# Feed-forward gate and up projections by a seven-product form over quarters of the operands

## The reference, cut to what matters

```
xn2 = rms_norm(h, norm2_w)                       # (512, 1024)
h   = h + (silu(xn2 @ w_gate) * (xn2 @ w_up)) @ w_down   # w_gate, w_up: (1024, 2816)
out = rms_norm(h, final_norm_w)
```

## Time and profile before

| | |
|---|---|
| median of the runs | 874.74 us |
| span of the profiled execution | 873.0 us (its own time is not listed apart; the median less the span is 1.74 us) |
| TensorE busy | 859.7 us, 98% |
| VectorE (DVE), ScalarE (ACT), GpSimd (POOL) busy | 34%, 36%, 39% |
| mean granted TensorE clock | 0.998 |

### The profile page before, as it was taken

How to read it: one execution, slowest core, us unless ns; L and a number is a source line. 1 busy time by engine, 2 the same in 40 slices (tenths; PEclk the granted TensorE clock), 3 DMA queues, 4 the chain that set the end, 5 groups by cost and what they waited for, 6 DMA issues and landing times.

```text
span 873.0 us, 10397 instructions
## 1 busy us (share of the span) xinstructions
PE 859.7 (98%) x4078; PEld 715.1 (82%) x4078; DVE 297.8 (34%) x304; ACT 314.4 (36%) x313; POOL 337.9 (39%) x80
## 2 busy tenths in 40 slices
PE   8999999999999999999999999999999999999996
PEld 7888888788788888888888898888888888888885
DVE  6374428563473912121212333000000000444445
ACT  3532445654655623232322553222222222222233
POOL 4444443214224244444444525444444444444440
PEclk9999999999999999999999999999999999999999
DMA  8842212212112132222225212222222222222212
GB/s 322 270 174 96 98 49 97 72 72 96 38 58 96 47 98 96 96 96 96 96 96 217 96 50 97 96 96 96 96 96 96 96 96 96 97 96 96 96 48 97
DMA packets 14658, 89.82 MB, mean 103 GB/s; under 512 B 1712, under 2 KB 1968, under 8 KB 5296
## 3 DMA queue, kind: packets, MB, share of 16 engines
q1 hardware_dynamic: 12384, 82.32, 26.1%
q10 hardware_dynamic: 2256, 7.24, 2.4%
HBM read 87.46 MB, written 2.10 MB: 103 GB/s over the span
## 4 chain that ended last, share of the span: by engine, by line
PE 92%; DVE 3%; ACT 2%; issue 1%; DMA 1%; POOL 0%; DVEq 0%; ACTq 0%; POOLq 0%
PE bank L849 19%; PE bank L851 19%; PE bank L850 19%; PE bank L868 9%; PE bank L867 9%; PE bank L866 9%; PE bank L1009 1%; PE bank L995 1%; PE bank L1003 1%; PE bank L965 1%; DVE vgs L649 1%; DMA par<-cols 1%; PE bank L895 0%; ACT w_hi L306 0%; PE bank L896 0%
## 5 line engine op out<-in xcount | busy, mean ns | idle before, releaser
L259 POOL TENSOR_TENSOR w_lo<-raw,w_hi 128x2048 fp32r<-128x2048 f32 x71 | 327.1, 4607 | 484.9 <-ACT w_hi L306 484.9
L849 PE MATMUL bank<-xt_hi,w_hi 128*128 128x512 f32 (+1 forms) x704 | 269.6, 383 | 3.2 <-ACT yb L406 1.5
L851 PE MATMUL bank<-xt_hi,w_lo 128*128 128x512 f32 (+1 forms) x704 | 267.1, 379 | 0.0
L850 PE MATMUL bank<-xt_lo,w_hi 128*128 128x512 f32 (+1 forms) x704 | 267.1, 379 | 0.0
L306 ACT ACTIVATE w_hi<-raw 128x2048 fp32r<-128x2048 f32 x72 | 137.7, 1912 | 297.3 <-PE bank L851 157.1
L849 PEld LDWEIGHTS bank<-xt_hi,w_hi 128*128 128x128 f32 x704 | 132.4, 188 | 29.5 <-issue 3.2
L850 PEld LDWEIGHTS bank<-xt_lo,w_hi 128*128 128x128 f32 x704 | 132.4, 188 | 25.8 <-issue 1.0
L851 PEld LDWEIGHTS bank<-xt_hi,w_lo 128*128 128x128 f32 x704 | 132.4, 188 | 25.1
L790 DVE TENSOR_TENSOR act<-bank,sil 128x512 f32 (+1 forms) x22 | 15.2, 692 | 199.2 <-PE bank L851 199.2
L795 DVE TENSOR_TENSOR al<-act,ah 128x1024 fp32r<-128x1024 f32 x11 | 51.7, 4700 | 60.2 <-ACT ah L504 60.2
L866 PE MATMUL bank<-w_hi,ah 128*128 128x512 f32 x176 | 68.5, 389 | 0.0
(11 more groups left out here) (175 smaller groups left out, 950.6 us busy)
## 6 DMA issues: line engine op xcount, KB each, us to landing
raw<-wstream SPq DMA_DIRECT2D x72, 1024.0 KB, 4.8
xw<-x_t SPq DMA_DIRECT2D x4, 512.0 KB, 8.2
h<-x ACTq DMA_DIRECT2D x1, 2048.0 KB, 7.8
out<-h SPq DMA_DIRECT2D x3, 512.0 KB, 2.6
raw<-wstream SPq DMA_DIRECT2D x2, 512.0 KB, 5.8
xn_in<-x SPq DMA_DIRECT2D x2, 512.0 KB, 12.0
xn_in<-x ACTq DMA_DIRECT2D x2, 512.0 KB, 4.3
vbias_bc<-vbias ACTq DMA_DIRECT2D x1, 1024.0 KB, 7.8
```

What stands on the lines that cost most here:

```text
L259: pool.tensor_tensor(w_lo[s][:, :], raw[s][:, :], w_hi[s][:, :], ALU.subtract).then_inc(lo_ready, 1)
L849: pe.matmul(dst, wh[:, k, cs], rh[:, k, ts], start=(k == 0), stop=False)
L850: pe.matmul(dst, wh[:, k, cs], rl[:, k, ts], start=False, stop=False)
L851: last = pe.matmul(dst, wl[:, k, cs], rh[:, k, ts], start=False, stop=(k == KD - 1))
```

## The change

The first pair stays as it was. For each of the other ten, the product of the weight pair W (read as 2 x 2 quarters: contraction halves k 0-3 and k 4-7, by the tiles of each of the two column groups) with the activations X (2 x 2 quarters: contraction halves by halves of 256 tokens) is made by Strassen's form in the variant with seven products. The operands are A11, A12, A22 (quarters of W) and the sums S1 = A21 + A22, S2 = S1 - A11, S3 = A11 - A21, S4 = A12 - S2; on the side of X, T1 = B12 - B11, T2 = B22 - T1, T3 = B22 - B12, T4 = B21 - T2 are formed once. A product is two column groups by four contraction steps by three matmuls, 24 matmuls of 256 columns; a pair is 7 x 24 = 168 of them where it was 96 of 512 columns.

The weight pair is loaded raw by two DMAs of 1024 KB each (k 0-3 and k 4-7 of both blocks, `k1_landed`, `k2_landed`) into `wp`, which takes the place of `raw[0]` and `raw[1]`. The sums are formed in PSUM: ACT copies A21 into banks 6-7 (`diff`), DVE forms S1, S2, S4 in banks 4-5 (`chain`) and S3 in `diff`. ACT makes seven high parts a pair, DVE the four low parts of the sums, POOL the three of the plain quarters. Each of the seven operands has one buffer. The results are joined from banks 0 to 3 by DVE (five additions of 512 columns) and ACT (two copies) into `cq`, ACT takes `silu` of the gate half, and POOL multiplies (`gated_pair`). Preparation runs one pair ahead: while TensorE makes pair p, the other engines prepare pair p+1, except S4, whose parts are made at the start of its own pair.

```
 SP
+sp.wait_ge(hi_ready, B_DOWN); sp.wait_ge(lo_ready, B_DOWN)
+pair_half(.., 0, k1_landed); pair_half(.., 1, k2_landed)
+with sp.Fori(1, PAIRS) as i:
+    sp.wait_ge(op_high, i*7 + (1-7)); sp.wait_ge(plain_low, i*3 + (1-3)); sp.wait_ge(s_formed, i*4 + (3-4))
+    pair_half(wstream[pair i], 0, k1_landed)
+    sp.wait_ge(op_high, i*7 + (6-7)); sp.wait_ge(plain_low, i*3); sp.wait_ge(s_formed, i*4)
+    pair_half(wstream[pair i], 1, k2_landed)
 TensorE
+def pair(p, first=False):        # first: further waits on the T operands and on the banks
+    pe.wait_ge(op_high, p*7 + (1-7)); pe.wait_ge(plain_low, p*3 + (1-3)); pe.wait_ge(taken, p*2 - 2)
+    product("A11", x11, 0, True)
+    pe.wait_ge(s_low, p*4 + (1-4)); pe.wait_ge(joined, p*5 - 5)
+    product("S1", t1, 2, True)
+    pe.wait_ge(s_low, p*4 + (2-4)); product("S2", t2, 1, True)
+    pe.wait_ge(s_low, p*4 + (3-4)); product("S3", t3, 3, True)
+    pe.wait_ge(plain_low, p*3 - 1); pe.wait_ge(taken, p*2 - 1)
+    product("A12", x21, 0, False)
+    pe.wait_ge(plain_low, p*3); pe.wait_ge(joined, p*5 + (2-5))
+    product("A22", t4, 3, False)
+    pe.wait_ge(s_low, p*4); pe.wait_ge(joined, p*5 + (3-5))
+    product("S4", x22, 2, False)
 DVE, pair(p) in order
+    join_c12(p-1); s_low_of("S4", chain, p*7)
+    form_s1(p*16 + 16, p + 1)     # waits for a21_copied and k2_landed of pair p+1
+    s_low_of("S1", ..); form_s2(); form_s3()
+    join_u2(p); s_low_of("S2", ..); join_u3(p); join_c22(p)
+    s_low_of("S3", ..); form_s4(); join_c21(p)
 ACT, pair(p) in order
+    s_high("S4", ..) after product 7(p-1); a21_copy(p*16 + 16); pair_silu(p-1); take_p1(p)
+    plain_high("A11"); s_high("S1") after product S1; s_high("S2") after S2; s_high("S3") after S3
+    take_c11(p); plain_high("A12"); plain_high("A22") after product A22
 POOL
+a11_low(1); a12_a22_low(5, 6); a11_low(7 + 1); a12_a22_low(7 + 5, 7 + 6)
+with pool.Fori(2, PAIRS) as p:
+    gated_pair(p-1, p-1); a11_low(p*7 + 1); a12_a22_low(p*7 + 5, p*7 + 6)
```

More of the change, by code:

```diff
@@ L489, in _ @@
             normalise_h(3)
[L490 to L501, removed]
+            split_turned(2)
@@ new lines, in _, with pair_silu @@
+            t_split(1, tb_hi[1][:, :, :])
+            t_split(2, tb_hi[2][:, :, :])
+            gate(0)
+            gate(1)
+            s_high("S2", chain, 2)
+            a.wait_ge(up_done, 2)
+            s_high("S3", diff, 3)
+            plain_high("A12", slice(4, 8), slice(0, P), k2_landed, 16)
+            t_split(3, xt_hi[:, 0:4, HT:SEQ])
+            plain_high("A22", slice(4, 8), slice(P, 2 * P), k2_landed, 16)
+            s_high("S4", chain, 4)
+            def pair_silu(n):
+                a.wait_ge(joined, n * 5)
+                a.wait_ge(taken, n * 2)
+                a.activation(silp[:, :, :], cq[:, :, 0, :], ACT.Silu).then_inc(silp_ready, 1)
@@ L780, in _ @@
             rstd_h(3)
[L781 to L791, removed]
+            weigh_turned(2)
@@ new lines, in quarter, with join_c22, join_c21 @@
+            def quarter(n, b, u):
+                return v.tensor_tensor(cq[:, n, :, :], bank[b][:, :].rearrange("p (g t) -> p g t", g=2),
+                                       u[:, :].rearrange("p (g t) -> p g t", g=2), ALU.add)
+            def join_c22(p, first=False):
+                if not first:
+                    v.wait_ge(pair_ready, p - 1)
+                v.wait_ge(joined, p * 5 + (2 - 5))
+                quarter(3, 2, u3).then_inc(joined, 1)
+            def join_c21(p):
+                v.wait_ge(product_done, p * 7 + (6 - 7))
+                quarter(2, 3, u2).then_inc(joined, 1)
@@ new lines, in join_c12, with pair @@
+            def join_c12(p):
+                v.wait_ge(product_done, p * 7)
+                quarter(1, 2, u2).then_inc(joined, 1)
+            def pair(p, first=False):
+                if not first:
+                    join_c12(p - 1)
+                    s_low_of("S4", chain, p * 7)
+                v.wait_ge(s_low, p * 4)
+                form_s1(p * 16 + 16, p + 1)
+                s_low_of("S1", chain, p * 7 + 2)
+                v.wait_ge(s_low, p * 4 + 1)
+                form_s2()
+                form_s3()
+                join_u2(p)
+                s_low_of("S2", chain, p * 7 + 3)
+                join_u3(p)
+                join_c22(p, first)
+                s_low_of("S3", diff, p * 7 + 4)
+                v.wait_ge(s_low, p * 4 + 2)
+                form_s4()
+                join_c21(p)
@@ L1070, in _ @@
                 tile_T(bank[2 + t][:, s1], wk(w_hi, 1), wk(w_lo, 1), t, xt_hi, xt_lo, s1).then_inc(up_done, 1)
[L1071 to L1078, removed]
-                    tile_T(bank[2 + t][:, :], wk(w_hi, 1), wk(w_lo, 1), t, xt_hi, xt_lo).then_inc(up_done, 1)
+            x11 = (xt_hi[:, 0:4, 0:HT], xt_lo[:, 0:4, 0:HT])
@@ L1082, in down @@
+            pair(1, True)
+            with pe.Fori(2, PAIRS + 1) as p:
+                pair(p)
             def down(m, s, first=False, last=False):
```

332 lines of the change are left out of this document (278 added, 54 removed).

## The result

The changed kernel takes 875.9 us (median of 20 runs, 875.29 to 876.62); before stands at 874.74 (20 runs, 874.63 to 874.85) on the same chip. Ratio 1.0014, 95% interval [1.0008, 1.0021]: some 0.14% slower, within what I had called no change, and on the other side of the forecast of 874.3. The profiled execution took 875.68 us with a span of 873.6, where before the span is 873.0. So 0.6 us of the profiled execution's difference lies inside the span. The rest is outside it: time minus span is 2.05 to 2.15 us in all 20 runs, against 1.74 before; I don't know why.

The account below looks back on a forecast made before the run. TensorE, busy 98% of the span, was taken to bound the kernel. Products and initial wait -16.8, ring +4.2, first pair's wait +10.0, clock +2.2 sum to -0.4 us: 874.3 us, own range 871.5 to 877, overall 867.5 to 884.

Parts of the forecast that it names:

- The first of the ten: Wait ahead of A22 in the first Strassen pair, whose successor's second weight half is loaded late: +10.0 us, bounds 7 and 12.
- the 1.74 us between time and span: Difference between median and profiled span before, carried over unchanged: span 872.6 became median 874.3 us.
- Products: TensorE's ten pairs: 168 matmuls at 0.120 us instead of 96 at 0.227, -16.1 us, and 0.7 us less initial wait.
- Engine loads: No side engine overfull per pair of 20.16 us: DVE 13.2, ACT 10.6, POOL 9.6 us.
- The ring: Loop from product A22 through reloading the single second-half weight buffer to next A22: 20.7 against 20.16 us, eight times, +4.2 us.
- The interpolation between transfers of other sizes with the same rows: Second weight half's 1024 KB transfer with 4 KB rows: 5.0 us between 3.6 and 7.8; 4.9 taken, bounds 4.7 and 6.
- The rival: Ring longer: the second half lands in 6 us, +9.9, 884.2 us; decides against the change from 5.2 us on; chance 0.28.
- the lock: POOL and DVE collide where DVE has both inputs in SBUF, for a whole instruction; costs only in the preparation, not the loop.
- The tile copies of `act`, S2, S3 come in time: First pair: S2 and S3 (533.6, 534.8) ready for products at 533.7 and 536.6, so no wait there.
- one of the prediction's signs of being wrong: PE waiting elsewhere than ahead of A22 (ahead of S1 or S4), a DVE PSUM pass over 1.3 us, or pace not 0.120.
- The clock: After the first pair's 10 us wait TensorE's clock is down for some twenty matmuls: +2.2 us, bounds 0 and 3.9.
- The chances: Forecast 0.46, ring not binding 0.25, ring longer 0.28, weight loads 0.01; hence faster 0.33, slower 0.35, no change 0.32.

Follow-up runs that it names:

- halves_before: Kernel before, with each 512-column matmul of the ten pairs made as two of 256: 887.78 us, ratio 1.0150.
- act_order: three_lock, with ScalarE in the first pair taking C11 and making A12's and A22's high parts right behind S1's, ahead of S2's and S3's: 859.83 us, 0.9835.
- rows8k: Changed kernel, with each weight half laid out as one 8 KB row per partition instead of two of 4 KB: 870.86 us, 0.9953.
- rows_lock: rows8k, with DVE's preparation order changed to keep instructions on two SBUF inputs away from POOL's: 867.35 us, 0.9923.
- four_edits: rows8k plus u3 ahead of S2's low part, first pair's joins ahead of next S1, and early A12/A22 high parts in the preparation: 871.4 us, 0.9961.
- five_edits: four_edits, with POOL instead of DVE making the low parts of T2 and T3 in the preparation: 868.45 us, 0.9926.
- three_lock: three_edits plus the DVE preparation order of rows_lock: 865.61 us (4 runs), 0.9887.
- three_edits: rows8k plus u3 ahead of S2's low part and the first pair's joins ahead of the next S1: 865.61 us (4 runs), 0.9900.

## Why the prediction was off, step by step

The forecast was 874.3 and the median came to 875.9. The step that failed is "The first of the ten": its +10.0 us of waiting measured 11.6. A second term was put at no change without a reason, the 1.74 us between time and span, which measured 2.1. Together they outweigh a forecast gain of 0.4 us.

- Products, -16.8: right. 2.88 us a product (pace 0.120), the first at 528.00 (forecast 527.97). halves_before confirms the 0.013 us at the upper clock, act_order the whole sum.
- Engine loads: right. DVE 1.22 us for 1024 columns from PSUM, ScalarE 1.03, POOL 2.44 as a mean with its stretched ones.
- The ring, +4.2: right in size and place (eight gaps, none in pair 10; 4.1 measured; from A22 to A22 20.67 us between pairs 2 and 9, forecast 20.7), but its inner terms made up for each other, which is luck. The landing was 5.5 instead of 4.9; the hops and the wait of DVE for itself were less, as DVE's timeline of one round shows:
```profile
609.43 1.23 DVE L951 TENSOR_TENSOR acc<-acc,wp 128x1024 f32<-128x1024 f32 x1 [3.94 <-DMA wp<-wstream]
611.75 1.23 DVE L964 TENSOR_TENSOR S_lo<-acc,S_hi 128x1024 fp32r<-128x1024 f32 x1 [1.09 <-ACT S_hi L588]
613.01 1.23 DVE L954 TENSOR_TENSOR acc<-acc,wp 128x1024 f32<-128x1024 f32 x1
...
617.01 0.68 DVE L1000 TENSOR_TENSOR u<-acc,u 128x512 f32<-128x512 f32 x1
```
S2's pass starts 0.03 us after S1's low part, not 0.24, and PE's A22 0.06 us after u3 (617.69 to 617.75), not 0.14. The interpolation between transfers of other sizes with the same rows was 0.6 us too low. The rival put the point from which the ring decides against the change at a landing of 5.2 us; by the forecast's own sum it is even at 4.94 (0.4 us over nine waits), and at 5.2 it is slower by more than 0.2%. With these hops 5.5 still left it near even.
- The first pair's wait, +10.0: this step failed, in size; the path was right. With product S1's wait it measured 11.6 us. The start of A22 was forecast at 552.4 and came at 554.03, by three terms: the second half of pair 1's own weights landed later than I had assumed and held DVE up (S3 ends 0.6 later); POOL's two low parts took 1.0 longer, since I looked at the lock only where POOL disturbs DVE and not where DVE's T4 part disturbs POOL; the transfer took 0.5 more; and against them the steps from S1 to PE took 0.4 less. rows8k took away the first and third (552.46); that this is so near the forecast 552.4 is luck too, since POOL's 1.0 us were still in it and were made up for by an earlier S3 (530.97, forecast 531.4) and shorter steps. rows_lock took away the second also, and the lock ahead of S2 (549.80).
- "The tile copies of `act`, S2, S3 come in time": wrong by 1.9 us at product S1, and by the prediction's own numbers: in pair 1 product S1 waits until DVE has made the first tile of `act`, which stands behind S3 in DVE's order (531.4), while the product was due at 530.85. A wait ahead of S1 was one of the prediction's signs of being wrong. The wait cost nothing of its own in the kernel as changed: A22's start was fixed by the load, and the products between merely came later. Where the wait for the load was shortened, it is a cost (four_edits, five_edits).
- The clock, +2.2 for twenty slow matmuls: 17 and 1.7 us. It fell some 3 us into the wait (2.4 of the 10 us to 550.00 are at the lower level, PE's last matmul having ended at 544.5) and came back 3.8 us into the work. A slow matmul cost 0.093 us more, not the 0.107 forecast: the distances at the lower clock are 0.213 us, which is 256 columns at 1.2 GHz and nothing beside, so the 0.013 us on top shows at the upper clock only. That the fall would come at a wait of 3.5 us (three_lock), and even of 2.8 (three_edits), in the midst of work I hadn't priced.
- The sum: 4.1 + 11.6 + 1.7 = 17.4 lost against 16.4 forecast, so +0.6 inside the span instead of -0.4; and 0.3 to 0.4 us outside the span, which the prediction had carried over from before; the median lies another 0.2 above the profiled execution. That turned a forecast of 0.05% faster into 0.14% slower. The balance of two terms of 17 us was too close for its sign to be told.
- The chances: 0.25 and a quarter of 0.46 make 0.37, not 0.33, and 0.28, 0.01 and a sixth of 0.46 make 0.37, not 0.35; so no change was left 0.27, not 0.32. It changes nothing in the forecast.

What stays open: the time outside the span. It is 2.1 us in act_order too, but 1.76 to 1.85 us in all five runs of five_edits, which has as many instructions (12270) and differs from four_edits (2.07 to 2.12) only in that POOL makes two of T's low parts, with a semaphore of their own. So the count of instructions isn't the cause; what is, these runs don't show.

## What to carry to other kernels

Fewer products of smaller tiles win less than the count says: take the fixed part of a matmul from rows at two sizes, and only then compare it with what the new dependencies can cost. When a change makes the bottleneck's work shorter, look for the single buffer whose way round (last reader, load, landing, first user) is now as long as the work; half a microsecond of it returned in every pass here, and each of the three ways tried to shorten it (a smaller transfer, longer rows, one instruction moved out of it) gave it all back. The first pass of such a pipeline deserves an order of its own on each engine: three edits to the steady state and the joins gave 1.0%, orders of DVE and ScalarE for the first pair alone made it 1.65%.

## What the runs showed of the hardware that I had not expected

- A load of 1 MB with two rows of 4 KB per partition lands in 5.5 us (5.2 to 9.1, 20 loads), with one row of 8 KB in 4.8 (4.7 to 6.9, 20 loads). The queue is the same, and so are the bytes; the two longest are those of pair 1, issued right behind another.
- GpSimd and VectorE hold each other up in both directions: 5.84 us instead of 4.79 (two of POOL's, one DVE instruction on two SBUF inputs amid them), 6.71 instead of 2.36 (two of DVE's beside two of POOL's).
- After a wait of 3.5 us in the midst of dense work 27 matmuls ran at the lower clock (three_lock), after one of 9.8 us 17 (the changed kernel), after 9.3 us 24 (rows8k), after 7.6 us 15 (rows_lock), and after one of 1.4 us none (act_order). Even the fall isn't ordered by the wait: a wait of 2.8 us brought it (three_edits, 16 slow ones, and only from the fifth matmul behind the wait on), one of 3.0 us did not (five_edits, ahead of product S1). Neither the longer wait nor the shorter one has the longer slow stretch, and what sets its length these runs don't show. The start of three_edits' stretch:
```profile
551.76 0.39 PE L1343 MATMUL acc<-xt_hi,A_hi 128*128 128x256 f32 x1 [2.56 <-ACT cq L626]
551.98 0.28 PE L1345 MATMUL acc<-xt_lo,A_hi 128*128 128x256 f32 x1
...
552.53 0.42 PE L1346 MATMUL acc<-xt_hi,A_lo 128*128 128x256 f32 x1
552.75 0.41 PE L1343 MATMUL acc<-xt_hi,A_hi 128*128 128x256 f32 x1
```
- A matmul of 256 columns took 0.120 us from start to start at the upper clock and 0.213 at the lower one (the changed kernel, 554.38 to 557.79): 1.78 times, not twice.
- VectorE's wait for its own last instruction took some 0.03 us here (S1's low part 611.75 + 1.23, S2's pass at 613.01), where the earlier trace rows had let me expect 0.24.
